# Memory values computed with the memory row on the partition, and their product with the probabilities in three fp32r products

## The reference, cut to what matters

```python
mkv = rms_norm(mem, mem_norm_g[l]) @ w_mem_kv[l]
mk, mv = jnp.split(mkv, 2, axis=-1)
y_c = memory_attention(ca_q.reshape(B, S, CA_HEADS, CA_HEAD_DIM),
                       mk.reshape(B, Mn, CA_HEADS, CA_HEAD_DIM),
                       mv.reshape(B, Mn, CA_HEADS, CA_HEAD_DIM))

def memory_attention(q, mk, mv):
    s = jnp.einsum('bshd,bmhd->bhsm', q, mk, preferred_element_type=jnp.float32) * CA_HEAD_DIM ** -0.5
    p = jax.nn.softmax(s, axis=-1)
    o = jnp.einsum('bhsm,bmhd->bshd', p.astype(mv.dtype), mv)
    return o.reshape(q.shape[0], q.shape[1], CA_WIDTH)
```

## Time and profile before

| | |
|---|---|
| median of 3 runs | 1328.13 us (1328.02 to 1328.16) |
| the profiled execution | 1327.76 us |
| its span, first to last instruction | 1326.0 us |
| tensor engine busy (PE) | 1307.4 us, 99% of the span |
| weight loads (PEld) | 1092.5 us, 82% |
| VectorE / ScalarE / GpSimd busy | 758.0 / 461.7 / 187.6 us |
| mean granted TensorE clock | 0.998 |

### The profile page before, as it was taken

One profiled execution on the slowest core, in us unless ns is written; L12 is line 12 of the kernel. 1 busy time (PEld: TensorE's weight loads), 2 busy tenths in 40 slices (PEclk: granted clock), 3 DMA queues, 4 the chain that ended last, 5 costly groups with the idle time before them and its releaser, 6 DMA issues.

```text
span 1326.0 us, 23795 instructions
## 1 busy us (share of the span) xinstructions
PE 1307.4 (99%) x10193; PEld 1092.5 (82%) x10193; DVE 758.0 (57%) x1278; ACT 461.7 (35%) x765; POOL 187.6 (14%) x128
## 2 busy tenths in 40 slices
PE   9999999999999999999999999999999999999997
PEld 8879988787788887888878888888888888888886
DVE  6786335576576576577965354555576522355335
ACT  5343433444353444343534331112433212222220
POOL 1023000013000023000331412233012200022000
PEclk9999999999999999999999999999999999999999
DMA  5155413221212232212223537653504333323321
GB/s 218 60 177 171 129 48 111 80 84 62 81 65 80 82 101 90 64 58 101 83 89 97 161 111 231 209 162 130 220 33 127 95 113 98 91 96 98 108 64 64
DMA packets 62832, 144.03 MB, mean 109 GB/s; under 512 B 5072, under 2 KB 28168, under 8 KB 62728
## 3 DMA queue, kind: packets, MB, share of 16 engines
q1 hardware_dynamic: 62728, 142.51, 33.2%
HBM read 127.79 MB, written 16.27 MB: 109 GB/s over the span
## 4 chain that ended last, share of the span: by engine, by line
PE 89%; DVE 6%; issue 2%; ACT 1%; DMA 1%; POOL 0%; SPq 0%; DVEq 0%; ACTq 0%; POOLq 0%
PE acc L1906 17%; PE acc L1908 16%; PE acc L1907 16%; PE ps_a L1907 2%; PE ps_a L1906 2%; PE ps_a L1908 2%; PE ps_a L2015 2%; PE ps_d L2093 2%; PE ps_d L2223 2%; PE ps_a L2223 2%; PE ps_d L2224 2%; PE ps_a L2225 2%; PE ps_a L2224 2%; PE ps_d L2225 2%; DVE w_lo L1407 1%
## 5 line engine op out<-in xcount | busy, mean ns | idle before, releaser
L1407 DVE TENSOR_TENSOR w_lo<-w_raw,w_hi 128x1024 fp32r<-128x1024 f32 x170 | 233.0, 1371 | 208.2 <-ACT w_hi L1105 207.5
L1105 ACT CAST w_hi<-w_raw 128x1024 fp32r<-128x1024 f32 x170 | 178.1, 1048 | 406.5 <-PE acc L1908 331.6
L1906 PE MATMUL acc<-n_hi,w_hi 128*128 128x512 f32 x744 | 303.3, 408 | 1.2 <-ACT conv_x L1180 1.2
L1908 PE MATMUL acc<-n_hi,w_lo 128*128 128x512 f32 x744 | 290.7, 391 | 0.0
L1907 PE MATMUL acc<-n_lo,w_hi 128*128 128x512 f32 x744 | 290.2, 390 | 0.0
L1906 PEld LDWEIGHTS acc<-n_hi,w_hi 128*128 128x128 f32 x744 | 139.9, 188 | 30.8 <-issue 3.8
L1908 PEld LDWEIGHTS acc<-n_hi,w_lo 128*128 128x128 f32 x744 | 139.6, 188 | 30.3
L1907 PEld LDWEIGHTS acc<-n_lo,w_hi 128*128 128x128 f32 x744 | 140.1, 188 | 25.8 <-issue 0.7
L1093 POOL TENSOR_TENSOR h_lo<-sq,h_hi 128x512 fp32r<-128x512 f32 x32 | 41.5, 1296 | 269.6 <-DVE h_hi L1822 269.6
L1906 PE MATMUL acc<-y_hi,w_hi 128*128 128x512 f32 x192 | 74.8, 390 | 0.0
L1908 PE MATMUL acc<-y_hi,w_lo 128*128 128x512 f32 x192 | 74.7, 389 | 0.0
(11 more groups left out here) (434 smaller groups left out, 2455.8 us busy)
## 6 DMA issues: line engine op xcount, KB each, us to landing
w_raw<-weights SPq DMA_DIRECT2D x200, 512.0 KB, 3.5
gate_scratch<-gate_st SPq DMA_DIRECT2D x24, 256.0 KB, 4.3
g_in<-gate_scratch SPq DMA_DIRECT2D x24, 256.0 KB, 3.9
y_raw<-y_scratch SPq DMA_DIRECT2D x16, 256.0 KB, 3.7
x_tok<-x SPq DMA_DIRECT2D x4, 512.0 KB, 5.3
y_scratch<-y_st SPq DMA_DIRECT2D x4, 512.0 KB, 2.7
y_scratch<-d_ET SPq DMA_DIRECT2D x4, 512.0 KB, 2.6
y_scratch<-y_st SPq DMA_DIRECT2D x8, 256.0 KB, 2.3
```

The lines of the kernel that those rows point to most:

```text
L1105: nc.scalar.copy(hi_of_tile(t), w_raw[:, t % RAW]).then_inc(hi_ready, 1)
L1407: V_.tensor_tensor(lo_of_tile(t), w_raw[:, t % RAW], hi_of_tile(t).bitcast(F32), ALU.subtract).then_inc(lo_ready, 1)
L1906: mm(bank, wh, hi_of(k), start=start and k == 0, stop=False)
L1908: last = mm(bank, wl, hi_of(k), start=False, stop=stop and k == KT - 1)
```

## The change

Tiles `mv` keep their places but are computed by `memory_values`: the memory rows (`m_hi`, `m_lo`) are stationary, the weights move, and the result has a memory row on the partition. Each half of a tile serves one half of the memory rows, 12 products of 512 columns for a tile. The first four tiles fill both banks of `acc`, the other four two banks of `ps_a`. Their loads take the weights in another pattern (pieces of 1 KB in place of 4 KB). After each group of four there is one cast to fp32r (ScalarE) and one subtraction (VectorE, `values_lo`). The two transpose steps go. The transposed probabilities are split too (`pT_hi`, `pT_lo`), and `cv` becomes twelve fp32r products of 512 columns. `mv_half0` lies where the position-bias strip lies, so the load of the strip waits for the `cv` of the second head. In the hand-written order `beta` goes from place 12 to place 11 on VectorE, ahead of the low split of tile 8, `mem_lo` from place 9 to place 12, and `decay` from 17 to 16.

```diff
-    out = [("mv", 0), ("mv", 1)]
+    out = []
-PE_AT = {4: (("ba_rows",),), 6: (("ba",), ("rows", ST), ("rows", ST + 1)), 14: (("bias",),), 17: (("decay",),)}
-ACT_AT = {4: (("ba",),), 7: (("rows", ST), ("rows", ST + 1)), 8: (("beta",),), 14: (("bias",),), 17: (("decay",),)}
-DVE_AT = {2: (("mem_norm",),), 6: (("beta_in",), ("mem_gain",)), 9: (("mem_lo",),), 12: (("beta",),)}
+PE_AT = {4: (("ba_rows",),), 6: (("ba",), ("rows", ST), ("rows", ST + 1)), 14: (("bias",),), 16: (("decay",),)}
+ACT_AT = {4: (("ba",),), 7: (("rows", ST), ("rows", ST + 1)), 8: (("beta",),), 14: (("bias",),), 16: (("decay",),)}
+DVE_AT = {2: (("mem_norm",),), 6: (("beta_in",), ("mem_gain",)), 11: (("beta",),), 12: (("mem_lo",),)}
...
+                    elif TILES[t][0] == "mv":
+                        g, kp = divmod(TILES[t][1], 4)
+                        first = weights[t_mv + 4 * g, :, 2 * kp]
+                        src = bass.AP(tensor=first.tensor, offset=first.offset,
+                                      ap=[[KT * P, P], [P * KT * P, 4], [1, 2 * P]])
...
                 elif step == 2:
                     sp.wait_ge(f_rep, 16)
+                    sp.wait_ge(a_mm, a_idx[("cv", HC // 2 - 1)] + 1)
...
-                    last = nc.scalar.copy(mv_T[:, j], bank[:, 0:MEM])
+                    last = nc.scalar.copy(mv_half[j // 4][:, 0], (acc[:], ps_a[:, 0:2])[j // 4])
...
+            def values_lo(g):
+
+                dve.wait_ge(acc_free, t_mv + 4 * g + 4)
+                V_.tensor_tensor(mv_half[g][:, 1], (acc[:], ps_a[:, 0:2])[g], mv_half[g][:, 0].bitcast(F32),
+                                 ALU.subtract).then_inc(mvl_ready, 1)
...
+                if kind == "ct":
+                    V_.tensor_tensor(pT_lo[:], ps_a[:, 0:2], pT_hi[:].bitcast(F32), ALU.subtract).then_inc(a_dve, 1)
...
+            def memory_values(t, j, n):
+
+                g, kp = divmod(j, 4)
+                mt = (n + t_mv) % 2
+                if n == 0:
+                    pe.wait_ge(lo_ready, t + 1)
+                if j == 0:
+                    pe.wait_ge(acc_free, t - 1 + n)
+                if j == 4:
+                    pe.wait_ge(f_sb, 1)
+                to = blocks((acc, ps_a)[g][:, mt])
+                for i in range(2):
+                    k = 2 * kp + i
+                    high, low = (m[:, k, mt * P:(mt + 1) * P] for m in (m_hi, m_lo))
+                    wh, wl = (view(flat(w), [[2 * P, 4], [1, P]], i * P) for w in (hi_of_tile(t), lo_of_tile(t)))
+                    mm(to, high, wh, start=k == 0, stop=False)
+                    mm(to, low, wh, start=False, stop=False)
+                    last = mm(to, high, wl, start=False, stop=k == KT - 1)
+                if n:
+                    last.then_inc(tile_used, 1)
...
-                            last = mm(ps_a[:, dt], mv_tok[:, mt, (2 * h + dt) * P:(2 * h + dt + 1) * P], pT_c[:, mt],
-                                      start=mt == 0, stop=mt == MT - 1)
+                            high, low = (mv_half[h // 2][:, n, mt, c:c + P] for n in range(2))
+                            mm(ps_a[:, dt], high, pT_hi[:, mt], start=mt == 0, stop=False)
+                            mm(ps_a[:, dt], high, pT_lo[:, mt], start=False, stop=False)
+                            last = mm(ps_a[:, dt], low, pT_hi[:, mt], start=False, stop=mt == MT - 1)
```

More of the change, by code:

```diff
@@ L169, in mixing_tiles @@
             need_free[("dz", 2 * p + i)] = ("dO", p - 1, 0)
-    for j in range(2 * HC):
-        need_free[("cq", j)] = ("mv", 1) if j < 4 else ("cs", j // 2 - 2)
+    for j in range(4, 2 * HC):
+        need_free[("cq", j)] = ("cs", j // 2 - 2)
     for h in range(HA):
@@ L238, in plan_order, with bank_free @@
         done[("LD", t)] = done[("ACT", "hi", t)] = done[("DVE", "lo", t)] = 0.0
-    old = lambda n: n >= n_first - 1
+    old = lambda n: n >= n_first - 1 and (tiles[n][0] != "mv" or tiles[n][1] % 4 == 3)
+    def bank_free(t):
+        if tiles[t][0] == "mv" and tiles[t][1]:
+            return []
+        if ("mv", KT - 1) in tiles[t - 2:t]:
+            return [("ACT", "evac", of[("mv", 3)]), ("DVE", "mv", 0)]
+        return [("ACT", "evac", t - 2)]
     for t in range(n_first, n_mix):
@@ L243, in plan_order @@
             add("PE", "main", ("main", t, a, b), (b - a) * (0.36 if short(t) else 0.681),
-                [("DVE", "lo", t), ("ACT", "evac", t - 2)] if n == 0 else [])
+                [("DVE", "lo", t)] + bank_free(t) if n == 0 else [])
     for t in range(n_first + SPL - 1, n_mix + SPL):
@@ L262, in plan_order @@
                 deps.append(("OUT", "gate", gate[gate.index(t) - 1]))
-            add("ACT", "evac", ("evac", t), 0.4 if short(t) else 0.65, deps)
+            add("ACT", "evac", ("evac", t), 1.05 if kind == "mv" else 0.4 if short(t) else 0.65, deps)
+            if kind == "mv":
+                add("DVE", "mv", ("mv", j // 4), 1.4, [("ACT", "evac", t)])
             if t in conv:
@@ L320, in plan_order @@
             deps = [("ACT", "attn", i - 1)] + [("DVE", "scale", j) for j in range(i) if attn[j][0] in SCALE_US][-1:]
-        if kind in ("mv", "cs", "av"):
-            deps.append(("ACT", "evac", of[{"mv": ("mv", KT - 1), "cs": ("cq", 2 * h + 1), "av": ("av", h)}[kind]]))
+        if kind in ("cs", "av"):
+            deps.append(("ACT", "evac", of[{"cs": ("cq", 2 * h + 1), "av": ("av", h)}[kind]]))
+        if i == 0:
+            deps.append(("DVE", "mv", 1))
         add("PE", "attn", ("attn", i), PE_US.get(kind, 0.87), deps)
@@ L337, in plan_order @@
     add("SP", "bias", ("bias", 1), 0.1, [("AT", 0)])
-    add("SP", "bias", ("bias", 2), 0.1, [("AT", 1)])
+    add("SP", "bias", ("bias", 2), 0.1, [("AT", 1), ("PE", "attn", a_idx[("cv", HC // 2 - 1)])])
     for kk in range(KT):
@@ L486, in build @@
         n_lo = sm("n_lo", [P, KT, S], F32R)
+        c1 = ExitStack()
+        mv_half = [sb_in(c1)("mv_half0", [P, 2, MT, 512], F32R)]
+        c1.close()
         strip = sm("strip", [P, HA, 2 * P])
@@ L566, in build @@
         cq_T = s3("cq_T", [P, 2, 2, S])
+        pT_lo = s3("pT_lo", [P, MT, S], F32R)
         c3.close()
@@ L660, in build @@
         lam_exp = sem("lam_exp")
+        mvl_ready = sem("mvl_ready")
         a_mm = sem("a_mm")
@@ L1187, in evacuate @@
                     last = nc.scalar.activation(gate_st[:], bank, ACT.Tanh, scale=0.5)
-                last.then_inc(acc_free, 1)
+                last.then_inc(acc_free, 4 if kind == "mv" else 1)
             def finish(t):
@@ L1205, in attn @@
                 act.wait_ge(a_mm, i + 1)
-                if kind == "mv":
-                    last = nc.scalar.copy(mv_tok[:, :, h * 512:(h + 1) * 512], ps_a[:, 0:2])
-                elif kind == "cs":
+                if kind == "cs":
                     act.wait_ge(a_max, n_max[i + 1])
@@ L1214, in attn @@
                 elif kind == "ct":
-                    last = nc.scalar.copy(pT_c[:], ps_a[:, 0:2])
+                    last = nc.scalar.copy(pT_hi[:], ps_a[:, 0:2])
                 elif kind in ("cv", "ay"):
@@ L1687, in _ @@
                         "pre": reload_hi, "beta_in": beta_and_decay_inputs, "beta": beta_and_decay,
-                        "mem_norm": memory_norm, "mem_gain": memory_gain, "mem_lo": memory_lo}
+                        "mv": values_lo, "mem_norm": memory_norm, "mem_gain": memory_gain, "mem_lo": memory_lo}
             for kind, *n in ORDER_OF["DVE"]:
@@ L1942, in first_tiles @@
                         last.then_inc(tile_used, 1)
+            def memory_values(t, j, n):
[17 more added lines that the diff above has]
+                    last.then_inc(tile_used, 1)
             def main_part(t, k0, k1):
-                kind = TILES[t][0]
+                kind, j = TILES[t]
+                if kind == "mv":
+                    memory_values(t, j, k0 // 4)
+                    return
                 if t < 2:
@@ L1966, in main_part @@
                     pe.wait_ge(lo_ready, t + 1)
-                    pe.wait_ge(acc_free, t - 1)
+                    if t - 2 <= t_mv + KT - 1 < t:
+                        pe.wait_ge(acc_free, t_mv + 4)
+                        pe.wait_ge(mvl_ready, 1)
+                    else:
+                        pe.wait_ge(acc_free, t - 1)
                 ks = range(k0, k1)
-                if kind in ("mk", "mv"):
+                if kind == "mk":
                     pe.wait_ge(su_lo2, len(LO2_ROWS))
@@ L1982, in attn @@
                         pe.wait_ge(a_dve, aD[i])
[L1983 to L1990, removed]
+                if kind == "cs":
                     pe.wait_ge(acc_free, TILES.index(("cq", 2 * h + 1)) + 1)
+                    pe.wait_ge(mvl_ready, 2)
                     for s in range(ST):
```

20 lines of the change are left out of this document (10 added, 10 removed).

## The result

| | before | after |
|---|---|---|
| median of 4 runs each | 1328.08 us (1327.47 to 1328.16) | 1335.63 us (1334.47 to 1336.61) |
| the profiled execution | 1327.76 us | 1335.21 us |
| its span | 1326.0 us | 1333.4 us |
| mean granted TensorE clock | 0.998 | 0.994 |

The kernel is slower by a little over half a per cent: ratio 1.0058, 95% interval 1.0046 to 1.007. The forecast was 1330.4 us with a range up to 1333.2; the time lies 2.4 us above the range. Three executions of two later kernels, a profiled one among them, ran at a much lower mean clock (1859 to 6167 us) and are left out of every median and of the reading of traces. In the changed kernel all lines move by 20 to 55: `bias` is L1913, the big products are L1934 to L1936, `mem_lo` is L1452, the doubling steps of DeltaNet's inverse are L2122 and L2124.

The account below looks back on a forecast made before the run. PE, the tensor engine, busy 99% of the span, was taken to bound the kernel. -5.7 + 0.2 + 8.8 - 2.7 + 1.7 = +2.3 us gave a median of 1330.4 us, 8-in-10 range 1326.8 to 1333.2.

Parts of the forecast that it names:

- The products: On PE, cheaper memory value and `cv` products and two transpose steps gone: 5.7 us less, bounds 5.3 and 6.2.
- The first `mv` tile: Its second half waits for the copy of the last `mk` tile: 0.2 us more, bounds 0 and 0.5.
- What was put at nothing: New casts, subtractions, 1 KB loads and the strip's load: no cost, with a bound of 1 us for queued weight loads.
- The wait at `bias`: PE idles at `bias` until 72.8 because VectorE finishes the `mem_lo` splits later: 8.8 us more.
- The old waits: PE's waits for the copy of tile 7 (1.24) and GpSimd's sums (1.43) go: 2.7 us less.
- The clock: PE's clock falls to half after the idle stretch at `bias`: 1.7 us more, bounds 0 and 3.4.
- the planner's new list: Rival: the order laid out anew behind tile 9 has other waits; 1 us either way, spread over all cases, no own chance.
- The sign: Direction of the whole kernel's change: slower 0.46, no change 0.43, faster 0.11.
- the old waits or a longer half clock: Rival: the 2.7 us of old waits stay (1333.1 us) or the half-pace stretch is twice as long (1332.1); chance 0.2.

Follow-up runs that it names:

- the shifted run: The changed kernel in its own order, with 64 fewer PE instructions at the start (512-column products replacing warm-up products): 1330.90 us, ratio 1.0016 to the kernel before.

## Why the prediction failed, step by step

- **The products, -5.7: right.** 0.227 and 0.226 us a product, the two transpose steps gone, and -6.2 for the whole kernel with the waits of before, of which 0.3 is issue waits.
- **The first `mv` tile, +0.2: nothing.** No wait; within its bounds.
- **What was put at nothing** (casts, subtractions, loads in 1 KB pieces, the strip's load): no new row in the waits view. Right.
- **The wait at `bias`, +8.8: right in mechanism, 9.2 by the row.** PE came 0.1 us earlier, and `bias` started 0.3 later than at 72.8: `beta` took 6.55 in place of 6.15 and began 0.15 earlier. The order alone, run by itself, is 8 us slower.
- **The old waits, -2.7: right.** Both are gone where the whole order is the new one and back where it is the old.
- **The clock, +1.7: right in mechanism, too small.** The low stretch lasted longer behind the restart than the start's; 2.4 is within the bounds of 0 and 3.4.
- **The step that failed is the last rival's**, "the planner's new list": "I allow 1 us either way". That was all the sum had for waits elsewhere, and it took them for waits between engines. The prediction says that PE's 18.6 idle us "must each be looked up", but the view of before had issue waits of 2.5 us, most of them in or right behind runs of 32x32 products, which it never named, and it took no account of PE's stream getting 192 instructions shorter. They became 5.7 us, one of them with half clock behind it: 4.7 us in all, by the shifted run, where 1 was allowed. With +0.7 on the clock, +0.4 at `bias` and -0.2 for the first `mv` tile that makes 5.6, against the 5.2 by which the forecast was short; 0.4 is left to the spread between runs.
- **The range** had room for the old waits or a longer half clock, but not for a stop. The sign was given as slower with 0.46 against 0.43 for no change, close to even. Without the stop the changed kernel is at 1330.90, ratio 1.0016, inside the 0.2% that the prediction calls no change. That this is only 0.5 from the forecast of 1330.4 is in part luck: with the misses of the other terms the sum would be 1331.3, and the executions of that kernel go from 1328.8 to 1332.3.

What is shown: the stop depends on the number of instructions ahead of it. It appears in the kernel before with 64 added and goes from three orders of the changed one with 192 added, from two of them also with 64 removed; it stays at its instructions when the time moves by 10 us; and it stands where a block of 256 ends, with a packet of 16 KB that starts 2.2 to 2.5 us before PE goes on. So PE stood waiting for its next instructions. Why the packet starts so late is not shown: the traces have its start and its length, not what asked for it. The Trainium skill ("Runtime: NRT & Kernel Launch", "Instruction fetch mechanics") says that instructions are refilled in blocks of 16 KiB, 256 instructions, strictly in sequence and on a DMA queue of the engine's own. The counts above agree. It also says that the fetch is hidden since instructions are issued more slowly than blocks are filled. That doesn't hold here: every usable trace has 2.2 to 5.7 us of issue waits without another cause, all but 0.2 us or so of it at block boundaries. The section gives PE 128 KiB for them in one place and two blocks in another; no run here shows how many it holds.

## What to carry to other kernels

When a step moves on one engine, list every wait elsewhere that counts it, and every transfer it issues: `mem_lo` three places later cost 9.2 us at `bias` and 2.4 of clock, and `bias` three places later held up SP's loads. When an edit changes how many instructions the bounding engine runs, its issue waits move as well; shift the count by 64 or 192 instructions, with work that leaves the rest of the schedule alone, before a difference of half a per cent is laid to the edit, or look in the trace whether an issue wait stands at a block boundary with a packet of the instruction queue just ahead of its end. Judge a product's worth with the order held fixed, then the order.

## What the runs showed of the hardware that was not expected

- PE can stop for 3.1 to 3.7 us inside a run of 32x32 products with nothing to wait for; it stands at a block boundary of its instruction stream and ends 2.2 to 2.5 us after a packet of 16 KB starts. 64 instructions fewer far ahead remove it, worth 4.5 to 4.7 us with the half clock behind it; 64 more in the kernel before bring it in, 5.6 us by the medians.
- After the idle stretch of 9.2 us the granted clock was 0.50 from just after 68 to just after 78 us, and 5 us of it lay behind the restart; after the one of 3.4 us it was 0.50 for 3.4 us, and for 6.8 in another kernel (518.3 to 525.2, the change in its old order).
- An idle stretch of 1.9 us was followed by 3.4 us at 0.50 as well (104.8 to 108.2, `bias` at 17), while the kernel before was at full clock behind its waits of 1.24 and 1.43 us.
- The clock also fell where PE was never idle: at 74.6 us after 3.1 us of 32x32 products, and at 12.0 us after 3.3 us of such products at the start. It didn't fall over 10.9 us of 104-column products in the same place.
